# Trainium2: the next group's first two convolution inputs are multiplied behind the last two chunks of the state-space scan

## What is computed

```python
def ssd_mixer(h, init_f, init_b, in_proj, conv_w, conv_b, dt_bias, a_log, d_skip, norm_g, out_proj):
    zxbcdt = h @ in_proj
    z, xbc, dt = jnp.split(zxbcdt, [D_INNER, D_INNER + CONV_DIM], axis=-1)
    xbc = jax.nn.silu(dwconv_centred(xbc, conv_w, conv_b))       # 5 taps
    x, bm, cm = jnp.split(xbc, [D_INNER, D_INNER + SSD_GROUPS * D_STATE], axis=-1)
    ...
    y_f, s_f = ssd_scan(x, dt[:, :, 0], a[0], bm, cm, init_f)
    y_b, s_b = ssd_scan(flip(x), flip(dt[:, :, 1]), a[1], flip(bm), flip(cm), init_b)
    y = y_f + flip(y_b) + x * d_skip.astype(F32)[:, None]
    y = rms_norm(y * jax.nn.silu(z), norm_g)
    return y @ out_proj, jnp.stack([s_f, s_b], axis=1)
```

## Time and profile before

| | us |
|---|---|
| median of 3 runs (lowest, highest) | 2040.35 (2037.51, 2043.9) |
| the profiled execution | 2038.09 |
| its span | 2036.2 |
| TensorE busy in the span | 1608.9 (79%) |
| mean granted clock of TensorE | 0.88 |
| the four groups of the scan, from the first conv input to the last `yd` | 908.6 to 1493.2, about 146 each |

### The profile page before, as it was taken

One profiled execution on the slowest core, in us unless ns is written; L12 is line 12 of the kernel. 1 busy time (PEld: TensorE's weight loads), 2 busy tenths in 40 slices (PEclk: granted clock), 3 DMA queues, 4 the chain that ended last, 5 costly groups with the idle time before them and its releaser, 6 DMA issues.

```text
span 2036.2 us, 17209 instructions
## 1 busy us (share of the span) xinstructions
PE 1608.9 (79%) x5763; PEld 852.0 (42%) x5763; DVE 644.6 (32%) x1045; ACT 567.5 (28%) x1111; POOL 264.5 (13%) x200
## 2 busy tenths in 40 slices
PE   3996899997549998169779879889879963899980
PEld 2443444443524443155345445444454433444430
DVE  2122566622300000323563563753750032000002
ACT  3002444411112221323353443542620010222211
POOL 0023000012300000400310310311210031000005
PEclk9998799998569999559989989989879975899995
DMA  9205445492179995331231231330260004799964
GB/s 363 84 0 154 162 170 186 161 293 72 48 280 345 357 350 208 104 96 49 94 93 41 93 95 40 113 114 0 90 251 0 0 11 167 279 357 351 355 243 155
DMA packets 192601, 326.99 MB, mean 161 GB/s; under 512 B 8962, under 2 KB 116946, under 8 KB 192534
## 3 DMA queue, kind: packets, MB, share of 16 engines
q1 hardware_dynamic: 173260, 270.29, 38.7%
q0 software_dynamic: 9232, 33.79, 4.6%
q10 hardware_dynamic: 10048, 22.19, 2.8%
HBM read 276.95 MB, written 49.28 MB: 160 GB/s over the span
## 4 chain that ended last, share of the span: by engine, by line
PE 57%; DMA 14%; issue 8%; DVE 7%; ACT 6%; POOL 5%; SPq 2%; ACTq 0%; DVEq 0%; POOLq 0%
PE ps L749 9%; PE ps L856 8%; PE ps L959 7%; DMA mem<-slot_rows 6%; PE ps L765 5%; DMA mem<-cum_rows 4%; PE ps L707 3%; PE ps L840 3%; PE ps L589 2%; PE ps L629 2%; PE ps L858 2%; PE ps L522 2%; PE ps L645 2%; PE ps L609 2%; DMA mem<-slot_rows,sloti 2%
## 5 line engine op out<-in xcount | busy, mean ns | idle before, releaser
L749 PE MATMUL ps<-mem 128*128 128x512 f32 x608 | 270.6, 598 | 0.0
L856 PE MATMUL ps<-mem 128*128 128x512 f32 x384 | 170.5, 597 | 2.5 <-ACT mem L1175 2.5
L1528 DVE TENSOR_TENSOR mem<-ps,mem 128x256 f32<-128x256 f32 x38 | 16.1, 425 | 490.5 <-ACT mem L1111 490.5
L749 PEld LDWEIGHTS ps<-mem 128*128 128x128 f32 x608 | 114.1, 193 | 129.4 <-issue 129.2
L840 PE MATMUL ps<-mem 128*128 128x512 f32 x320 | 149.2, 621 | 0.0
L765 PE MATMUL ps<-mem 128*128 128x512 f32 x304 | 138.6, 599 | 3.8 <-ACT mem L1115 3.8
L959 PE MATMUL ps<-mem 128*128 128x512 f32 x320 | 137.5, 592 | 0.0
L1583 DVE SCALAR_TENSOR_TENSOR mem<-mem 128x642 f32<-128x642 f32 x96 | 85.2, 888 | 138.7 <-ACT mem L1197 128.3
L741 PE MATMUL ps<-tab,mem 128*128 128x128 f32 x304 | 44.0, 292 | 88.3 <-DMA mem<-slot_rows 86.0
L589 PE MATMUL ps<-mem 128*128 128x512 f32 x240 | 107.1, 605 | 7.2 <-DMA mem<-in_attn_w_qkv 7.2
L513 PE MATMUL ps<-tab,mem 128*128 128x128 f32 x160 | 32.6, 378 | 99.6 <-DVE mem L1287 63.9
(11 more groups left out here) (284 smaller groups left out, 2277.7 us busy)
## 6 DMA issues: line engine op xcount, KB each, us to landing
mem<-in_mod_w SPq DMA_DIRECT2D x24, 2048.0 KB, 7.9
mem<-in_expert_w_gate SPq DMA_DIRECT2D x38, 1024.0 KB, 7.2
mem<-in_expert_w_up SPq DMA_DIRECT2D x38, 1024.0 KB, 10.7
mem<-in_expert_w_down SPq DMA_DIRECT2D x38, 1024.0 KB, 10.4
mem<-cum_rows SPq DMA_DIRECT2D x40, 512.0 KB, 4.3
mem<-slot_rows SPq DMA_DIRECT2D x38, 512.0 KB, 9.6
slot_rows<-mem ACTq DMA_DIRECT2D x38, 512.0 KB, 7.6
slot_rows<-mem SPq DMA_DIRECT2D x1, 13312.0 KB, 46.1
```

Of the source, the lines that this page charges most:

```text
L749: last = nc.tensor.matmul(ps[:, 2 + j, :], XGT[j][:, k, :], WS[j][:, k, :], start=(k == 0), stop=(k == KD - 1))
L856: nc.tensor.matmul(ps[:, b, :], w[:, k, :], HT[:, k, SEQ:TOK], start=(k == 0), stop=(k == KD - 1))
```

## The change

The six conv inputs of a group come in the order x0, x1, B, C, x2, x3. Those of step 0 and 1 of group `g + 1` are multiplied in group `g`, behind the `yd` of chunks 3 and 4. For that ACT reads the last gate product out one chunk earlier. PE's loop is written out instead of `Fori`. PE now turns x0 at `st` = 2, x1 at 3, B at 4, x2 at 6, x3 at 7, each time waiting for ACT's copy of the one before; ACT copies them out at its steps 3, 4, 5, 7, 8. The x weights are issued first at the start, and the gate weights wait for four conv inputs instead of two.

```diff
+        CONV_ORDER = [("x", 0), ("x", 1), ("bc", 0), ("bc", 1), ("x", 2), ("x", 3)]
...
+            x_weights(0)
             bc_weights(0)
-            x_weights(0)
...
-                sp.wait_ge(s_ip, g * 6 + 3)
+                sp.wait_ge(s_ip, g * 6 + 5)
...
-            with pe.Fori(0, SG) as g:
+            def conv_input(g, i):
+                if i == 0:
+                    pe.wait_ge(s_wx, g * 16 + 16)
+                    pe.wait_ge(s_zs, g * 5 + 1)
+                if i == 2:
+                    pe.wait_ge(s_wbc, (g + 1) * 32)
+                if i >= 2:
+                    pe.wait_ge(s_u, g * 6 + i - 1)
+                kind, m = CONV_ORDER[i]
+                w = (WX if kind == "x" else WBC)[:, :, m * P:(m + 1) * P]
+                b = 2 * (i % 2)
+                for k in range(KD):
+                    nc.tensor.matmul(ps[:, b, :], w[:, k, :], HT[:, k, SEQ:TOK], start=(k == 0), stop=(k == KD - 1))
+                for k in range(KD):
+                    last = nc.tensor.matmul(ps[:, b + 1, 0:SEQ], w[:, k, :], HT[:, k, 0:SEQ],
+                                            start=(k == 0), stop=(k == KD - 1))
+                last.then_inc(s_ip, 1)
+
+            for i in range(2):
+                conv_input(0, i)
+            for g in range(SG):
...
-                for st in range(8):
+                turned = 0
+                for st in range(2, 8):
                     if st < 6:
...
+                        conv_input(g, st)
                     if st in (5, 7):
                         gate_product((st - 5) // 2)
...
+                    kind, m = CONV_ORDER[st - 2]
+                    if (kind, m) != ("bc", 1):
+                        pe.wait_ge(s_sl, g * 6 + st - 1)
+                        if turned == 0:
                             pe.wait_ge(s_y, g * 5 + 1)
                             pe.wait_ge(s_cbm, g * 5 + 1)
...
+                        else:
+                            pe.wait_ge(s_txe, g * 5 + turned)
+                        src = BT if kind == "bc" else CVT[m % 2]
...
+                        turned += 1
...
                     last.then_inc(s_yd, 1)
+                    if cc >= NT - 2 and g + 1 < SG:
+                        conv_input(g + 1, cc - (NT - 2))
...
-                    if st == 3 or 5 <= st:
-                        a = st - 3
-                        act.wait_ge(s_tx, g * 5 + max(a - 1, 0) + 1)
-                        dst = XT[:, :, (a - 2) * P:(a - 1) * P] if a > 0 else BK
+                    if st in (3, 4, 5, 7, 8):
+                        kind, m = CONV_ORDER[st - 3]
+                        act.wait_ge(s_tx, g * 5 + (3, 4, 5, 7, 8).index(st) + 1)
+                        dst = XT[:, :, m * P:(m + 1) * P] if kind == "x" else BK
...
-                    act.wait_ge(s_z, g * 5 + cc + 2)
-                    act.wait_ge(s_yq, g * 5 + max(cc - 1, 0) + 1)
-                    nc.scalar.activation(ZS[cc % 2], ps[:, cc % 4, :], ACT.Silu).then_inc(s_zs, 1)
+                    if cc < NT - 1:
+                        gate_out(cc)
+                    if cc == NT - 2:
+                        square(cc - 1)
+                        gate_out(NT - 1)
                     if cc + 1 < NT:
                         less_sums(cc + 1)
-                    if cc >= 1:
+                    if cc >= 1 and cc != NT - 2:
                         square(cc - 1)
```

More of the change, by code:

```diff
@@ L842, in gate_product @@
                     last.then_inc(s_z, 1)
-                pe.wait_ge(s_zs, g * 5 + 1)
-                for st in range(8):
+                turned = 0
+                for st in range(2, 8):
                     if st < 6:
[L847 to L860, removed]
+                        conv_input(g, st)
                     if st in (5, 7):
                         gate_product((st - 5) // 2)
[L863 to L867, removed]
+                    kind, m = CONV_ORDER[st - 2]
+                    if (kind, m) != ("bc", 1):
+                        pe.wait_ge(s_sl, g * 6 + st - 1)
+                        if turned == 0:
                             pe.wait_ge(s_y, g * 5 + 1)
                             pe.wait_ge(s_cbm, g * 5 + 1)
-                        if r >= 1:
-                            pe.wait_ge(s_txe, g * 5 + r)
-                        src = CVT[a % 2] if a > 0 else BT
+                        else:
+                            pe.wait_ge(s_txe, g * 5 + turned)
+                        src = BT if kind == "bc" else CVT[m % 2]
                         for t in range(NT):
@@ L1194, in _ @@
                         act.wait_ge(o_u, g * 6 + st + 1)
-                        ch = (g + 16 + 4 * st) if st < 2 else (g * 4 + st - 2)
+                        kind, m = CONV_ORDER[st]
+                        ch = (g * 4 + m) if kind == "x" else (g + 16 + 4 * m)
                         nc.scalar.activation(AC2[st % 2], U[st % 2][:, 2:2 + AW], ACT.Identity,
@@ L1202, in _ @@
                         act.wait_ge(s_cv, g * 6 + a + 1)
-                        if 4 <= a:
-                            act.wait_ge(s_tx, g * 5 + a - 2)
-                        dst = (BT, CT)[a] if a < 2 else CVT[a % 2]
+                        kind, m = CONV_ORDER[a]
+                        if kind == "x" and m >= 2:
+                            act.wait_ge(s_tx, g * 5 + m - 1)
+                        dst = (BT, CT)[m] if kind == "bc" else CVT[m % 2]
                         nc.scalar.activation(dst[:, SEQ:TOK], AC2[a % 2][:, 0:DEC], ACT.Silu)
                         nc.scalar.activation(dst[:, 0:SEQ], AC2[a % 2][:, DEC + 2:DEC + 2 + SEQ], ACT.Silu).then_inc(s_sl, 1)
-                    if st == 3 or 5 <= st:
-                        a = st - 3
-                        act.wait_ge(s_tx, g * 5 + max(a - 1, 0) + 1)
-                        dst = XT[:, :, (a - 2) * P:(a - 1) * P] if a > 0 else BK
+                    if st in (3, 4, 5, 7, 8):
+                        kind, m = CONV_ORDER[st - 3]
+                        act.wait_ge(s_tx, g * 5 + (3, 4, 5, 7, 8).index(st) + 1)
+                        dst = XT[:, :, m * P:(m + 1) * P] if kind == "x" else BK
                         nc.scalar.activation(dst, psf[:, 2048:2048 + TOK].rearrange("p (t n) -> p t n", t=NT), ACT.Copy)\
@@ L1237, in less_sums, with gate_out @@
                     last.then_inc(s_less, 1)
+                def gate_out(t):
+                    act.wait_ge(s_z, g * 5 + t + 2)
+                    act.wait_ge(s_yq, g * 5 + max(t - 1, 0) + 1)
+                    nc.scalar.activation(ZS[t % 2], ps[:, t % 4, :], ACT.Silu).then_inc(s_zs, 1)
                 less_sums(0)
```

## The result

| | before | changed |
|---|---|---|
| median of 12 runs, us (lowest to highest) | 2040.66 (2035.96 to 2051.32) | 2055.78 (2051.45 to 2063.46) |
| ratio, 95% interval | | 1.0072 (1.0054 to 1.0090) |
| profiled execution's span, us | 2036.2 | 2049.5 |
| first conv input to last `yd`, us | 584.8 | 592.8 |

The kernel became 0.7% slower, some 15 us (11 to 18 by the interval). The forecast was 12.9 us.

A forecast was written before the change was run, and what follows sets the result against it. TensorE was taken to bound the kernel, with some 21 us of holes per group. Terms -27.1 + 28.0 - 6.4 + 18.4 = +12.9 us gave a median of 2053.3 us, range 2048 to 2057, held at 60%.

The forecast's parts named there:

- Part 1, the filled hole: Before the last chunk's `yo` at three group borders: a next-group conv input fills PE's 7 us hole, gaining 27.1 us.
- the tie that the text had named: At the last chunk: DVE ends the weight tile at 1199.67, `yd` would start at 1199.7, so just ready.
- signs of being wrong: Clock kept at 1.00 across the transpose holes; ACT's copy earlier; new border wait on `s_u` or L1626 over 0.5 us.
- Part 2, the first copy of the next group: Third conv input waits for ACT's first copy; both come 8.5 us behind `yd`, a stall of 0 to 0.3 us.
- Part 3, the transposes: Behind conv inputs 3 and 4, PE waits 3.5 us for ACT's copy, eight times: a loss of 28.0 us.
- The saved hole: End of the convolution part: x2 turned behind the first gate product removes a hole, 1.6 us per group, 6.4 in all.
- The clock: Behind the eight transpose holes TensorE falls to 1.2 GHz for some us: 2.3 us each, 18.4 in all.
- The rival in which they keep it: The eight transpose stalls come but keep the full clock: 5.5 us gained, 2034.9 us; chance 10%.
- each time: On TensorE, holes a little over 3 us cost the clock every time; the short 1.51 us hole costs only itself.
- upper bound of 2.8 us a hole: Clock loss at most 2.8 us behind each of eight transpose holes, from 2.7 us read at group 1's end; total 2057.3.

## Why the prediction was right, by its steps

**Part 1, the filled hole.** Forecast 27.1 us. The three borders gave 9.5, 9.8 and 6.6 (second conv input against the end of chunk 3's `yd`, before and after), 25.9 together; taking the fill out cost 28.3 at the same borders. The border 2 to 3 gave 1.2 less than forecast, because there `yd` waited 0.95 us for DVE's weights, the tie that the text had named. A wait there of more than 0.5 us was also one of its signs of being wrong: at one border of three it came, at a price of 1 us. ACT's moved SiLU was not the cause: it ended before the sums for `less_sums` had landed, after which ACT still idled 1.89 us. It was the DMA: from its issue to `less_sums` it took 7.9 us (issued at 1338.98), and 6.4 at the same place of the kernel before (1328.02 to 1334.39):

```profile
1344.38 0.60 ACT L1254 ACTIVATE mem<-ps 128x512 f32<-128x512 f32 x1
1346.87 2.45 ACT L1247 ACTIVATE mem<-mem,small 128x128 f32<-128x128 f32 x8 [1.89 <-DMA mem<-cum_rows]
```

**Part 2, the first copy of the next group.** Forecast 0 to 0.3 us. ACT's square ends at 1073.88 in group 0 of the changed kernel, its table load begins at 1073.89, the first copy at 1075.18, and conv input 2 follows the second one without a hole:

```profile
1073.89 1.28 ACT L1200 ACT_TABLE_LOAD   x1
1075.18 0.60 ACT L1200 ACTIVATE mem<-ps 128x512 f32<-128x512 f32 x1
```

The 1.38 us of draining beside each load that the Trainium skill gives (ScalarE: Activation LUTs, What ACT_TABLE_LOAD costs) do not show between these rows, and the 4 us that it would have added did not come. The measurement decides here.

**Part 3, the transposes.** Forecast 3.5 us for each of eight stalls; the trace has 3.42 of idle each, and a transpose starts 3.6 later than it would have: 28.7 us. The saved hole gave 1.7 us per group (2.22 between the starts of the two transposes, less 0.55), 6.7 in all. The clock was forecast at 2.3 us each, 18.4 in all; the eight places of the changed kernel's trace lose 1.6 to 3.0 us each, 2.0 in the mean, 16 in all (transposes and conv input against 0.71 and 7.03), and keeping PE busy gave back 15.6. So this term was a little too large, and its reason right: all eight holes lost the clock. The rival in which they keep it, with a gain of 5.5 us, fell on exactly this. But "each time" is more than the kernels show: without the fill two of eight holes just as long kept it, and in the kernel with the later transposes a hole of 2.05 us was followed by a gate product of 8.73 instead of 7.03. The length of the hole alone doesn't decide. That all eight lost it here, and the term came to 16.0 and not to the 12.5 of the kernel without the fill, the rows before could not have told. The conv input behind a hole was to take 9 to 11 us; it took 8.0 to 9.4, and the text's own 2.3 us would have made it at most 9.3. Its upper bound of 2.8 us a hole is likewise a little above the 2.7 that it reads from the rows, 0.6 us in the sum.

**The sum** of the measured terms is -25.9 + 28.7 - 6.7 + 16.0 = +12.1 us, by the trace, against 12.9. The terms missed by 1.2, 0.7, 0.3 and 2.4 us and cancelled in part, so the mechanism and the signs were right, and the closeness of the totals is some luck. The scan as a whole grew by 8.0 in the profiled execution. The last chunk of group 3, which has no fill, accounts for 3.2 of the difference: its `yo` waited 5.55 us there and 7.04 in the profiled execution of before, and `yo` and `yd` behind it took 5.4 and 7.1. That hole lies between 5.0 and 7.4 in the nine traces. The remaining 5.3 of the profiled 13.3 lie outside the scan, in code that the change does not touch; ahead of the scan, for instance, work that is the same in all of them let the first conv input start between 904.7 and 915.7 us in the nine profiled executions. So a single profile can't carry a difference of a few us, and the 15 us of the medians are to be read with their interval of 11 to 18.

**What stayed open.** Why two holes of 3.42 us kept the clock in one kernel, and why the DMA of the sums takes 6.0 us in one place and 8.2 in another, no run shows. ACT's early SiLU was not run by itself. Whether the order x, x, B, C, with its copies repaired, is better than the old order with the fill isn't decided either: its convolution parts are 7 us shorter (249.3 against 256.4), which is the four holes of 1.6 us that the old order keeps, but the scans are alike (554.9 and 550.9 against 554.6), and the medians of 2011 and 2018 come from different series.

## What to carry to other kernels

An engine's ordered stream is a timetable. When work moves to another step on one engine, look on every engine that answers it for the step in which the answer comes; here the answer came one wait too late, and moving one copy in ACT's stream, or the transposes on PE, turned a loss of 0.7% into a gain of 1.8 or 1.9%. Count a hole of some 3 us on TensorE twice, once as idle time and once as clock, but only where TensorE sets the pace, and as a price that is mostly paid, not always (8 of 8 here, 6 of 8 without the fill). Where two traces differ in a part that no edit touches, compare the part that it does. A change of several parts is best run part by part: the part that was meant to bring the gain brought it, and one that came along with it cost more.

## What the runs showed of the hardware

A TensorE that has nothing useful to do for 3.4 us can be better off multiplying something: eight stretches of thrown-away products, 29 us of work in all, made the convolution parts 15.6 us shorter and the kernel 17 us faster by the medians, because the real products behind them ran at 2.4 GHz throughout instead of partly at 1.2. The same between the chunks, where the chain of DMA, ACT and DVE comes last, brought nothing.

The length of a hole doesn't settle the clock by itself: holes of 3.42 us lost it 14 times in 16 (8 of 8 in the changed kernel, 6 of 8 without the fill), and behind one of 2.05 us it fell too, to a mean of 0.57 over the next 3.8 us.
